# Three PSUM banks in turn for the shared jobs of an attention stage

## The reference, cut

```python
# windowed heads, per block of 128 queries: keys of this block and the one before
s = einsum(q, k) * dh ** -0.5
logits = where(valid, s + bias, NEG_INF)
# softmax over the logits and one sink, then times v

# picked heads, per block of 128 queries
dots = einsum('bqhd,bsd->bqhs', iqb, ik) * (IDX_DIM ** -0.5)
score = einsum('bqh,bqhs->bqs', iwb, relu(dots))
_, idx = top_k(where(causal, score, NEG_INF), topk)      # topk = 256
q_lat = einsum('bthd,hcd->bthc', q, w_uk) * (dh ** -0.5)
logits = einsum('bqhc,bqkc->bhqk', ql, c_kv[idx]) + bias
o = einsum('bhqk,bqkc->bqhc', softmax(logits), c_kv[idx])
out = einsum('bqhc,hcd->bqhd', o, w_uv)
```

## Time and profile before

| | us |
|---|---|
| three runs | 3460.64, 3464.9, 3465.06; median 3464.9 |
| profiled execution | 3475.4 |
| its span | 3473.6 |
| PE busy | 3150.6 (91%) |
| DVE busy | 1399.9 (40%) |
| ACT busy | 918.1 (26%) |
| POOL busy | 814.5 (23%) |
| mean granted clock of PE | 0.934 |

### The profile page before, as it was taken

How to read it: one execution, slowest core, us unless ns; L and a number is a source line. 1 busy time by engine, 2 the same in 40 slices (tenths; PEclk the granted TensorE clock), 3 DMA queues, 4 the chain that set the end, 5 groups by cost and what they waited for, 6 DMA issues and landing times. The chain is left out here.

```text
span 3473.6 us, 40801 instructions
## 1 busy us (share of the span) xinstructions
PE 3150.6 (91%) x16622; PEld 2538.7 (73%) x16622; DVE 1399.9 (40%) x2837; ACT 918.1 (26%) x1571; POOL 814.5 (23%) x330
## 2 busy tenths in 40 slices
PE   5987888876989997999999989999979999999997
PEld 4864455554958896888888856888859788888886
DVE  4045788884321544222222273213554522222226
ACT  3222354544122312111111133114431511211211
POOL 3110000004221024333333323231112222222223
PEclk9995698887989998999999999999989999999999
DMA  5222100112221011111111131110020211111112
GB/s 127 64 61 86 61 25 25 37 38 62 69 95 44 19 49 43 49 48 48 48 48 48 49 130 37 49 40 14 14 103 25 73 43 49 48 48 48 48 49 97
DMA packets 178760, 187.76 MB, mean 54 GB/s; under 512 B 24731, under 2 KB 147483, under 8 KB 178236
## 3 DMA queue, kind: packets, MB, share of 16 engines
q1 hardware_dynamic: 169696, 174.05, 16.2%
q10 hardware_dynamic: 8924, 11.74, 1.1%
HBM read 172.09 MB, written 13.68 MB: 53 GB/s over the span
## 5 line engine op out<-in xcount | busy, mean ns | idle before, releaser
L2616 POOL TENSOR_TENSOR weights_parts<-weights,weights_parts 128x2048 fp32r<-128x2048 f32 (+3 forms) x97 | 436.3, 4498 | 1166.0 <-ACT weights_parts L1332 1166.0
L711 PE MATMUL psum<-x_cols_parts,weights_parts 128*128 128x512 f32 x1552 | 610.1, 393 | 23.8 <-POOL weights_parts L2616 13.6
L713 PE MATMUL psum<-x_cols_parts,weights_parts 128*128 128x512 f32 x1552 | 607.9, 392 | 0.0
L713 PE MATMUL psum<-weights_parts,region_parts 128*128 128x512 f32 (+1 forms) x1120 | 410.0, 366 | 0.0
L711 PEld LDWEIGHTS psum<-x_cols_parts,weights_parts 128*128 128x128 f32 x1552 | 294.2, 190 | 88.0 <-issue 11.9
L711 PE MATMUL psum<-weights_parts,region_parts 128*128 128x512 f32 x864 | 337.2, 390 | 6.9 <-DVE region_parts L2570 5.8
L713 PEld LDWEIGHTS psum<-x_cols_parts,weights_parts 128*128 128x128 f32 x1552 | 294.0, 189 | 61.8
L712 PE MATMUL psum<-weights_parts,region_parts 128*128 128x512 f32 x864 | 336.9, 390 | 0.0
L1332 ACT ACTIVATE weights_parts<-weights 128x2048 fp32r<-128x2048 f32 (+2 forms) x98 | 181.8, 1855 | 582.2 <-DMA region<-in_bup_h_dram 142.6
L711 PE MATMUL psum<-weights_parts,x_cols_parts 128*128 128x256 f32 (+1 forms) x832 | 241.7, 290 | 29.3 <-DVE x_rows L2102 12.7
L712 PE MATMUL psum<-wide_parts,weights_parts 128*128 128x512 f32 x616 | 241.3, 392 | 0.0
(11 more groups left out here) (371 smaller groups left out, 5224.8 us busy)
## 6 DMA issues: line engine op xcount, KB each, us to landing
weights<-in_ada_w_dram SPq DMA_DIRECT2D x24, 1024.0 KB, 5.2
weights<-in_ffn_up_w_dram SPq DMA_DIRECT2D x42, 512.0 KB, 4.5
weights<-in_w_up_dram SPq DMA_DIRECT2D x16, 1024.0 KB, 5.1
weights<-in_w_down_dram SPq DMA_DIRECT2D x16, 1024.0 KB, 5.1
weights<-in_m_in_w_dram SPq DMA_DIRECT2D x12, 1024.0 KB, 5.3
weights<-in_ffn_down_w_dram SPq DMA_DIRECT2D x10, 1024.0 KB, 5.0
weights<-in_xa_wkv_dram SPq DMA_DIRECT2D x4, 2048.0 KB, 8.1
weights<-in_m_in_w_dram SPq DMA_DIRECT2D x3, 2048.0 KB, 8.6
```

Source lines behind the costliest of these rows:

```text
L711: pe.matmul(o, lhsT=a_hi, rhs=b_hi, start=(first and i == 0), stop=False)
L713: m = pe.matmul(o, lhsT=a_lo, rhs=b_hi, start=False, stop=(last and i == len(terms) - 1))
L2616: pool.tensor_tensor(WLO[buf][:, 0:width], WRAW[buf][:, 0:width], WHI[buf][:, 0:width], ALU.subtract).then_inc(s("w_lo"), 1)
```

## The change

Shared jobs of slots g < 7 and of slots g >= 41 take banks 7, 5 and 3 in turn (by the job's number modulo 3); those between stay in bank 7. `job_banks` gives the ring of a slot, `U_BANK` the bank of a job, `U_AT` how many jobs used that bank before, `U_COUNT` how many there are per bank (151 in bank 7, 28 in bank 5, 29 in bank 3), `U_EARLY` how many of them belong to the first region (16 each). `u_free` becomes three semaphores, one per bank. A job waits for as many copies from its own bank as jobs used it before.

Where a wait used the single count to mean "this job and all before it", it now names the jobs: both queries in `sparse_logits`, all four a_log in `window_max`, both index pieces in `index_sum`. At the borders of the two regions there are waits between the shared jobs and the heads that use banks 3 and 5. Every instruction stands in the order in which it stood before, on every engine; the banks and the waits are what changes.

```diff
--- before.py
+++ after.py
@@ -129,6 +129,25 @@
         if _place in shared_jobs(*_slot):
             UJ[shared_jobs(*_slot)[_place]] = len(UJ)
 N_UJ = len(UJ)
+
+
+def job_banks(n, i):
+
+    g = NH * n + i
+    return EARLY_BANKS if g < EARLY_END else LATE_BANKS if g >= LATE_AT else (7,)
+
+
+EARLY_BANKS, LATE_BANKS, EARLY_END, LATE_AT = (7, 5, 3), (7, 5, 3), 7, 5 * NH + 1
+U_BANK, U_AT, U_COUNT, U_EARLY = {}, {}, {3: 0, 5: 0, 7: 0}, {}
+for _slot in A_SLOTS:
+    for _place in PLACES:
+        if _place in shared_jobs(*_slot):
+            _job, _ring = shared_jobs(*_slot)[_place], job_banks(*_slot)
+            U_BANK[_job] = _ring[UJ[_job] % len(_ring)]
+            U_AT[_job] = U_COUNT[U_BANK[_job]]
+            U_COUNT[U_BANK[_job]] += 1
+    if NH * _slot[0] + _slot[1] == EARLY_END - 1:
+        U_EARLY.update(U_COUNT)
 
 
 def build_program(nc, I, out):
@@ -355,7 +374,7 @@
 
         f_ready, f_free, t_ready, t_free = s("f_ready"), s("f_free"), s("t_ready"), s("t_free")
         w_in = [s("w_in0"), s("w_in1")]
-        u_ready, u_free = s("u_ready"), s("u_free")
+        u_ready, u_free = s("u_ready"), {b: s(f"u_free{b}") for b in U_COUNT}
         rows_in, cols_in, own_dve, own_act = s("rows_in"), s("cols_in"), s("own_dve"), s("own_act")
 
 
@@ -538,7 +557,8 @@
                                      ).then_inc(s("vb_out"), 16)
 
             def mods_out(n):
-                sp.wait_ge(u_free, UJ[("ada", 3 * n + 2)] + 1)
+                job = ("ada", 3 * n + 2)
+                sp.wait_ge(u_free[U_BANK[job]], U_AT[job] + 1)
...
@@ -558,7 +578,8 @@
...
-            sp.wait_ge(u_free, N_UJ)
+            for b in U_COUNT:
+                sp.wait_ge(u_free[b], U_COUNT[b])
...
@@ -828,9 +849,19 @@
 
             def shared(job):
 
-                if UJ[job] > 0:
-                    pe.wait_ge(u_free, UJ[job])
-                return PS[:, 7, :]
+                b, at = U_BANK[job], U_AT[job]
+                if at > 0:
+                    pe.wait_ge(u_free[b], at)
+                if b == 3 and at == 0:
+                    pe.wait_ge(s("ix0_e"), NH)
+                if b == 3 and at == U_EARLY[3]:
+                    pe.wait_ge(s("d_e"), LATE_AT - 1)
+                if b == 5 and at == U_EARLY[5]:
+                    pe.wait_ge(s("d_te"), LATE_AT - 1)
+                return PS[:, b, :]
+
+            def freed(job):
+                pe.wait_ge(u_free[U_BANK[job]], U_AT[job] + 1)
 
             def window_logits(m, e):
                 o, c0 = shared(("a_log", m, e)), ORDER[m]
@@ -852,7 +883,7 @@
 
             def window_out(m, b):
                 o, c0 = shared(("a_out", m, b)), ORDER[m]
-                pe.wait_ge(u_free, UJ[("a_t", m, b)] + 1)
+                freed(("a_t", m, b))
                 for h in (2 * b, 2 * b + 1):
                     kts = (1,) if c0 == 0 else (0, 1)
                     for kt in kts:
@@ -883,7 +914,10 @@
 
             def sparse_logits(g):
                 n = g // NH
-                pe.wait_ge(u_free, UJ[("query", n, 1)] + 1)
+                freed(("query", n, 0))
+                freed(("query", n, 1))
+                if g == NH + 1:
+                    pe.wait_ge(u_free[3], U_EARLY[3])
                 if g >= 2:
                     pe.wait_ge(s("d_e"), g - 1)
                 else:
@@ -903,6 +937,8 @@
                 pe.wait_ge(s("d_n"), g + 1)
                 if g >= 1:
                     pe.wait_ge(s("d_te"), g)
+                if g == NH:
+                    pe.wait_ge(u_free[5], U_EARLY[5])
                 for kt in range(ORDER[g // NH] + 1):
                     ins = pe.transpose(PS[:, 4 + kt // 4, (kt % 4) * P:(kt % 4) * P + P], LG[:, g % 2, kt * P:kt * P + P], ident[:, :])
                 ins.then_inc(s("d_t"), 1)
@@ -945,7 +981,8 @@
                     sparse_values(g - 2)
                 for place in ("ix1", "turned", "ada", "query1"):
                     job(place)
-            pe.wait_ge(u_free, N_UJ)
+            for b in U_COUNT:
+                pe.wait_ge(u_free[b], U_COUNT[b])
...
@@ -1468,7 +1505,7 @@
             def empty_shared(job):
                 kind = job[0]
                 act.wait_ge(u_ready, UJ[job] + 1)
-                o = PS[:, 7, :]
+                o = PS[:, U_BANK[job], :]
                 if kind == "a_t":
                     m, b = job[1:]
                     if ORDER[m] == 0:
@@ -1496,7 +1533,7 @@
                     if n >= 2 and part == 0:
                         act.wait_ge(s(f"mods_out{n % 2}"), 64 * (n // 2))
                     ins = act.activation(modr[:, n % 2, part, :], o[:, 0:ADA_Q], ACT.Copy)
-                ins.then_inc(u_free, 1)
+                ins.then_inc(u_free[U_BANK[job]], 1)
 
             L = (ORDER[1] + 1) * P
             for h in range(NH):
@@ -1544,7 +1581,8 @@
                 if i == 4 and 0 <= n + 1 < NT:
                     window_exp(n + 1)
             split_block(WO0)
-            act.wait_ge(u_free, N_UJ)
+            for b in U_COUNT:
+                act.wait_ge(u_free[b], U_COUNT[b])
...
@@ -2003,13 +2041,16 @@
             def window_scores(m, e):
                 w0, h0 = P if ORDER[m] == 0 else 0, 4 * (e // 2) + e % 2
                 dve.wait_ge(u_ready, UJ[("a_log", m, e)] + 1)
-                v = PS[:, 7, :].rearrange("p (a b) -> p a b", a=2)
+                b = U_BANK[("a_log", m, e)]
+                v = PS[:, b, :].rearrange("p (a b) -> p a b", a=2)
                 dve.scalar_tensor_tensor(SB[:, h0:h0 + 3:2, w0:], v[:, :, w0:], DH ** -0.5,
-                                         bias[:, h0:h0 + 3:2, w0:], ALU.mult, ALU.add).then_inc(u_free, 1)
+                                         bias[:, h0:h0 + 3:2, w0:], ALU.mult, ALU.add).then_inc(u_free[b], 1)
 
             def window_max(m):
                 w0 = P if ORDER[m] == 0 else 0
-                dve.wait_ge(u_free, UJ[("a_log", m, 3)] + 1)
+                for e in range(4):
+                    job = ("a_log", m, e)
+                    dve.wait_ge(u_free[U_BANK[job]], U_AT[job] + 1)
                 mark(dve.tensor_reduce(mx, SB[:, :, w0:], AX.X, ALU.max))
                 settled()
                 mark(dve.tensor_tensor(mx, mx, sink, ALU.max))
@@ -2029,7 +2070,9 @@
                 if k == 1:
                     dve.wait_ge(s("ix0_e"), h + 1)
                 else:
-                    dve.wait_ge(u_free, UJ[("ix", k, h, (L - 1) // BW)] + 1)
+                    for c in range((L - 1) // BW + 1):
+                        job = ("ix", k, h, c)
+                        dve.wait_ge(u_free[U_BANK[job]], U_AT[job] + 1)
                 if h == 0:
                     dve.tensor_scalar(score[:, k % 2, 0:L], RL[:, 0, 0:L], iwt[:, b, 0:1], None, ALU.mult).then_inc(s("ix_s"), 1)
                 else:
```

## The result

| | before | after |
|---|---|---|
| median of the runs | 3462.8 us (3460.6 to 3465.1) | 3420.1 us (3417.6 to 3422.6) |
| profiled execution (span) | 3475.4 us (3473.6) | 3422.6 us (3420.8) |

The ratio is 0.9877, with a 95% interval of 0.986 to 0.9894: **faster by 42.7 us**. The prediction said 3432 us, range 3422 to 3452. Of the runs in the experiments, two that were in a slow state (5699.4 us of the kernel before, 6865.0 us of E4) are left out of every median.

A forecast was written before the change was run, and what follows sets the result against it. TensorE, idling on bank 7's turns and mostly at 1.2 GHz, was taken to set the early slots' pace; early ring 30.3 us plus late ring 3.0 made 33.3 off the 3464.9 us median: 3432 us, range 3422 to 3452.

The forecast's parts named there:

- The waits named: Slots 0 to 6: waits of L867, L874, L850 and L841 for copies out of bank 7 would be gone.
- slower rival: Stage 1: TensorE misses its clock rise and stays at 1.2 GHz, net 6 us slower, 3471 us; chance 0.04.
- no gain: Rival: ACT's copies are late, three banks fill, TensorE waits as before; 0 to 5 us gained, 3462 us; chance 0.06.
- The clock at 1.2 GHz: Rival: early-ring clock stays low, only the turns and start are saved, 17.3 us, 3448 us; chance 0.15.
- the clock up and down: Rival: TensorE overtakes DVE, waits and falls back; slots 1 to 3 take 9 us each, 3436 us; chance 0.20.
- slots 1 to 3 at 7.5 us: Early ring at 2.4 GHz: these slots take 22.5 us together instead of 39.46, saving 17.0 us.
- unbroken run of four groups: Slots -1 to 1: a_t, ada, sparse logits and a_out without waits between them raise the clock near 297 us.
- slots 4 and 5: Early ring: DVE's 14.98 us with window_exp's wait on top, 18.0 us, saving 3.7 us.
- low end: Range's fastest time, 3422 us: 43.1 us gained, with slots 1 to 3 at 6.4 us each and late turns entirely gone.
- The start: Before slot 0: banded logits issued ahead and query in its own bank bring first sparse logits 1.6 us earlier.
- Stage 5 on: Late ring, 772 to 826 us: turns of 3.5 us, taken as 3.0 us saved; nothing in stage 5 itself.
- The added waits: Extra waits in sparse logits, index_sum and window_max: taken as 0 us, upper bound 2.4 us on DVE.

The follow-up runs named there:

- E4: Kernel before (bank 7 alone) plus one unread identity matmul ahead of each shared job's wait in slots 0 to 3; 3453.6 us, ratio 0.9963.
- E11: The kernel before, unchanged, run once more for a second profile; one run, 3457.5 us.
- E9: Kernel before (bank 7 alone) plus two unread identity matmuls ahead of each shared job's wait in slots -1 to 3; 3455.3 us, ratio 0.9957.
- E5: Changed kernel, but in the early ring each a_t and ada job also waits for the copy of the job just before it; 3434.3 us, ratio 0.9897.
- E8: Changed kernel with both rings cut to bank 7, keeping every added wait and count; 3461.3 us, ratio 0.9983 against the kernel before.
- E1: Changed kernel with only the early ring: three banks up to slot 6, bank 7 alone from slot 7 on; 3433.2 us, ratio 0.9898.
- E10: Changed kernel with bank 7 alone before slot 0; three banks in slots 0 to 6 and from slot 41; 3428.2 us, ratio 0.9888.
- E12: The changed kernel, unchanged, run once more for a second profile; one run, 3426.5 us.

## Why the prediction was right and wrong

**Right in kind.** The waits named are gone in slots 0 to 6, and L943's for the exponentials stays. The clock rose at 296.2 us, where 297 was forecast, and stood at 1.00 over all of slots 1 to 3, with L898 at 1.12 us. Stage 1 begins 40 us earlier and takes 91.9 us (93.4 before), so the slower rival is out. So is "no gain". The clock at 1.2 GHz and the clock up and down did not happen in slots 1 to 3 either: there were 30 us at the upper level without a break, up to the wait for the exponentials. The Trainium skill, page "TensorE: Matmul & The Clock Gate", section "A second HAM failure mode: psum-queue depth-cycling", describes a kernel that cycles through banks, idles briefly between its groups and swings between the levels. Here the small idles and the short rises went with one bank (0.60 in E11), and three banks in turn gave 1.00. The same page's section "HAM oscillation — how this bites in real kernels" reports that in one kernel, rearranged so that TensorE stayed at its upper level, double-buffered PSUM gave no further gain. Here TensorE stood at its lower level, and E4 and E9 show that filling its idles with unread work raises the clock.

**The step that failed: slots 1 to 3 at 7.5 us.** I had TensorE at 33.70 x 0.55, or 6.2 us a slot, DVE at 5.8, and added 1.3 for two equal engines that take turns, from DVE's 0.87 in stage 1. They measured 5.80 each, 5.1 us less together. Both parts were too big. TensorE did the same work in 17.41 us, 0.52 of 33.70. And with free banks between them the two engines work ahead of each other instead of taking turns: 17.41 and 16.89 of 17.41 us busy. The share that DVE reaches in stage 1, which has one bank, did not carry over to slots that have three. The same error is in slots 4 and 5 (18.0 forecast, 15.33 measured, 2.7 us), where the wait for the exponentials was added although DVE covers it. The other terms held: slot 0 12.7 (13.3), slot 6 15.6 (15.5), slot 7 10.0 (10.3).

**The reason for the rise** was only half right. Its time was hit to 1 us, but E5 cuts the unbroken run of four groups and the clock still rises, at 303.6 instead of 296.2 us. That the idles held the clock down is shown by E4 and E9; whether they count as a whole or by the runs that they leave is not.

**Why the time lies outside the range.** The gain, 42.7 us, is inside the 13 to 43.1 us that the range was made of. The range was set off from the median of three runs, 3464.9; the four runs of the result have 3462.8 for the same kernel, 2.1 us less, and the miss is 1.9 us. The low end had slots 1 to 3 at 6.4 us each, where they took 5.8, another 1.8 us.

**The baseline was not a typical one.** The sum was made against a profile whose slots 0 to 7 were 6.7 us longer than the mean of four (108.2 and 101.5). The 10.5 us between that execution and the median were taken off both sides as if they lay elsewhere. The two errors nearly cancel: against the mean profile, slots 0 to 7 gave 101.5 - 71.0 = 30.5 us (the forecast, less its start, was 28.7). That nearness is luck: the forecast had these slots end up at 79.5 us, and they took 71.0.

**The terms against typical executions.** Slots 0 to 7: 30.5 us. The start: slot 0's reduction stands at 290.9 us on average in the four profiles with one bank up to slot 7 and nothing filled, at 288.4 in the five with three banks from slot -8 on, 2.5 (forecast 1.6). Stage 5 on: 50.5 against 46.2 by the means of the six profiles without the late ring and the eight with it, 4.2 (forecast 3.0). Sum 37.2. Behind the attention: 2651.6 against 2646.6 by the means of seven each, 5.0 (forecast nothing). Together 42.2 of the 42.7 measured. That is no close check: slots 8 to 48, left out of it, take 362.9 to 373.1 us from one execution to another, 367.6 and 368.0 by the means of seven each. Had these 5 us not come, the time would have been inside the range; with slots 1 to 3 sized right its low end would have been 3420.0, and the 3420.1 measured just inside. The sizing is understood; where the 5 us come from is left open above.

**The added waits** cost nothing that shows (E8), as taken.

## What to carry to other kernels

Where one buffer makes a fast engine idle for well under a microsecond before each job, look at the granted clock first: here the idles themselves were 12.7 of 101 us, and the clock that they held down was worth more (some 18 of the 30.5 us of slots 0 to 7, an estimate by subtraction). A cheap test is to fill the idles with work that nobody reads. Once buffers let two engines run ahead of each other, forecast the slot as the longer of their works, with no charge for turns, and take a second profile of the kernel before when its profiled execution lies away from the median.

## What was not expected of the hardware

- TensorE with turns of 0.58 to 0.78 us did not always stay at 1.2 GHz: the same kernel spent slots 1 to 3 at 0.50 in one execution and at 0.60 in another, and slots 0 to 7 took 108.2 or 97.7 us.
- With the ring the stretch repeats to 0.01 us (17.41 us in the change, E1, E10 and E12), though its start moved by 3.4 us between executions (287.36 and 290.76).
- An idle of 3.4 us was followed by 27 us at 1.2 GHz with TensorE busy 26.37 of 27.10 us; the clock did not come back at once with the work.
- TensorE's work in slots 1 to 3 took 0.52 of its time at the lower level, closer to the ratio of the two levels than the 0.54 that single groups show (1.12 and 2.07 us).
